# Turning attention probabilities by VectorE and 16 transfers a head in place of TensorE's transposes

## The reference

```python
s = einsum('nbqhd,nbkhd->nbhqk', qb, kk) * HEAD_DIM**-0.5 + bias   # masked to the window
p = exp(s - max(s)); den = sum(p)
o = einsum('nbhqk,nbkhd->nbqhd', p, vv) / den
# groups merged by their denominators, then
y = o * silu(z);  x = x + y @ w_out;  out = rmsnorm(x, final_norm)
```

## Time and profile before

| | us |
|---|---|
| median of 3 runs (1427.52 to 1428.34) | 1427.92 |
| the profiled execution, its time | 1427.84 |
| its span in the trace | 1426.0 |
| TensorE busy in the span | 1414.5 (99%) |
| VectorE / ScalarE / GpSimd busy | 866.0 / 705.3 / 387.2 |

### The profile page before, as it was taken

How to read it: one execution, slowest core, us unless ns; L and a number is a source line. 1 busy time by engine, 2 the same in 40 slices (tenths; PEclk the granted TensorE clock), 3 DMA queues, 4 the chain that set the end, 5 groups by cost and what they waited for, 6 DMA issues and landing times.

```text
span 1426.0 us, 22807 instructions
## 1 busy us (share of the span) xinstructions
PE 1414.5 (99%) x8515; PEld 1256.6 (88%) x8515; DVE 866.0 (61%) x1417; ACT 705.3 (49%) x999; POOL 387.2 (27%) x171
## 2 busy tenths in 40 slices
PE   8999999999999999999999999999999999999997
PEld 8999999988888888888888888888888888888886
DVE  3999999632544444446666666666656666666523
ACT  6444444675644444445454545444444544545543
POOL 6888888888300000000000000000000000001595
PEclk9999999999999999999999999999999999999999
DMA  9766766655757557569676676666577666574662
GB/s 283 195 183 187 195 180 192 193 177 180 242 202 254 201 198 253 196 201 265 191 196 183 172 194 197 184 184 185 164 207 194 177 185 185 161 220 151 229 207 88
DMA packets 401023, 279.06 MB, mean 196 GB/s; under 512 B 6731, under 2 KB 355483, under 8 KB 400588
## 3 DMA queue, kind: packets, MB, share of 16 engines
q1 hardware_dynamic: 400492, 277.47, 65.9%
q10 hardware_dynamic: 480, 0.90, 0.2%
HBM read 267.79 MB, written 10.55 MB: 195 GB/s over the span
## 4 chain that ended last, share of the span: by engine, by line
PE 98%; ACT 1%; DMA 0%; DVE 0%; issue 0%; POOL 0%; POOLq 0%; ACTq 0%
PE bank L423 14%; PE bank L419 14%; PE bank L447 10%; PE bank L449 10%; PE bank L448 10%; PE bank L422 7%; PE bank L420 7%; PE bank L427 6%; PE bank L428 6%; PE bank L429 6%; PE bank L1521 1%; PE bank L1559 1%; PE bank L1413 1%; PE bank L1539 0%; PE bank L1544 0%; ACT mem_a L699 0%
## 5 line engine op out<-in xcount | busy, mean ns | idle before, releaser
L365 POOL TENSOR_TENSOR w_lo<-raw,w_hi 128x1024 fp32r<-128x1024 f32 x159 | 382.7, 2423 | 1013.1 <-ACT w_hi L356 1013.0
L356 ACT ACTIVATE w_hi<-raw 128x1024 fp32r<-128x1024 f32 x254 | 268.4, 1061 | 326.4 <-PE bank L449 192.5
L394 DVE TENSOR_TENSOR w_lo<-raw,w_hi 128x1024 fp32r<-128x1024 f32 x224 | 272.2, 1223 | 111.6 <-ACT w_hi L388 109.1
L388 ACT ACTIVATE w_hi<-raw 128x1024 fp32r<-128x1024 f32 x224 | 236.5, 1058 | 155.1 <-PE bank L423 147.1
L427 PE MATMUL bank<-mem_a,w_hi 128*128 128x256 f32 x768 | 216.1, 281 | 1.8 <-DVE mem_a L1012 1.6
L428 PE MATMUL bank<-mem_a,w_hi 128*128 128x256 f32 x768 | 214.4, 279 | 0.0
L429 PE MATMUL bank<-mem_a,w_lo 128*128 128x256 f32 x768 | 213.4, 278 | 0.0
L423 PE MATMUL bank<-mem_b,w_hi 128*128 128x512 f32 x512 | 202.5, 396 | 0.0
L419 PE MATMUL bank<-mem_b,w_hi 128*128 128x512 f32 x512 | 202.3, 395 | 0.0
L365 DVE TENSOR_TENSOR w_lo<-raw,w_hi 128x1024 fp32r<-128x1024 f32 x96 | 117.6, 1226 | 135.0 <-ACT w_hi L356 134.9
L447 PE MATMUL bank<-w_hi,mem_a 128*128 128x512 f32 x504 | 196.5, 390 | 0.0
(11 more groups left out here) (195 smaller groups left out, 2106.6 us busy)
## 6 DMA issues: line engine op xcount, KB each, us to landing
raw<-b_w_in_dram SPq DMA_DIRECT2D x128, 512.0 KB, 4.3
raw<-w_kv_dram SPq DMA_DIRECT2D x48, 1024.0 KB, 7.0
raw<-w_kv_dram SPq DMA_DIRECT2D x96, 512.0 KB, 5.5
raw<-a_w_in_dram SPq DMA_DIRECT2D x47, 1024.0 KB, 5.8
raw<-a_w_out_dram SPq DMA_DIRECT2D x16, 1024.0 KB, 5.0
raw<-b_w_out_dram SPq DMA_DIRECT2D x16, 1024.0 KB, 5.0
v_dram<-v_stage SPq DMA_DIRECT2D x12, 512.0 KB, 3.4
v_rows<-v_dram SPq DMA_DIRECT2D x15, 384.0 KB, 5.8
```

The lines of the kernel that those rows point to most:

```text
L356: nc.scalar.activation(w_hi[:, stream.half_slot(half), :], raw[:, slot, part:part + HALF], ACT.Copy).then_inc(hi_done, 1)
L365: eng.tensor_tensor(w_lo[:, stream.half_slot(half), :], raw[:, slot, part:part + HALF], w_hi[:, stream.half_slot(half), :].bitcast(F32), A ...
L394: nc.vector.tensor_tensor(w_lo[:, QKV.half_slot(half), :], raw_half(half), w_hi[:, QKV.half_slot(half), :].bitcast(F32), ALU.subtract).the ...
```

## The change

Each 128 x 512 row half of `prob` is transposed by VectorE in squares of 32 by 32 into a new tile `prob_sq`. Squares that lie off the diagonal of a block are then on the wrong partitions; 16 transfers a head (`MOVES`), one for each pair of a source and a destination group of 32 partitions, write them back into `prob` at their place. Each is 32 partitions x 2 halves x 512 bytes, 32 KB. ACT and DVE then make `prob_hi` and `prob_lo` in four pieces of 128 columns from `prob` in SBUF, and TensorE reads the other groups' probabilities from `prob` itself in four runs of 32 columns. `prob_t`, the PSUM copies and the separate `v_last` go. The attention trails by one head less: `attend(h-1)` stands at the end of head h, and two heads are peeled.

```diff
+PEELED = 2
+SQUARE = 32
+SQUARES = P // SQUARE
+MOVES = SQUARES * SQUARES
...
+        def turned_probs(t, block):
+            return prob[:, t, :].rearrange("p (i b s) -> p b i s", i=SQUARES, b=BLOCKS)[:, block, :, :]
...
@@ SP
+            def move_squares(h):
+                sp.wait_ge(squares_turned, TT * (h + 1))
+                for i in range(SQUARES):
+                    for j in range(SQUARES):
+                        row = BLOCKS * SQUARE
+                        sp.dma_start(prob[j * SQUARE:(j + 1) * SQUARE, :, i * row:(i + 1) * row],
+                                     prob_sq[i * SQUARE:(i + 1) * SQUARE, :, j * row:(j + 1) * row]
+                                     ).then_inc(prob_turned, 16)
...
                     load_half(sp, h, half, w[:, tiles, bass.ds(cols[half // 2], P)])
+                    if half == NG:
+                        move_squares(h - 2)
...
                     load_slab(sp, B_OUT, c, q, out_slab(b_w_out[0], c, q))
+                    if (c, q) == (0, 0):
+                        move_squares(HEADS - 2)
                     if (c, q) == (0, B_OUT.per_turn - 1):
-                        sp.wait_ge(attended, HEADS - 2)
-                        load_v(HEADS - 2, (HEADS - 2) * P)
-                        sp.wait_ge(scores_done, HEADS)
-                        sp.dma_start(v_last, v_dram.ap()[:, :, :, (HEADS - 1) * P:]).then_inc(v_last_in, 16)
+                        sp.wait_ge(attended, HEADS - 1)
+                        load_v(HEADS - 1, (HEADS - 1) * P)
+                        move_squares(HEADS - 1)
                         sp.wait_ge(resid_stored, 16)
                         sp.dma_start(resid[:, :, :], resid_dram.ap()).then_inc(resid_in, 16)
@@ ACT: slab step 6 of head h, after copy_lower(h, 3) and before head_hi(h)
+            def probs_hi(h):
+                act.wait_ge(prob_turned, 16 * MOVES * (h + 1))
+                for u in range(TT):
+                    for t in range(TT):
+                        nc.scalar.activation(of_squares(prob_hi[:, u, t * P:(t + 1) * P]),
+                                             turned_probs(t, SAME if t == u else CROSS), ACT.Copy).then_inc(prob_his, 1)
@@ ACT: after head 15
-            y2_his(range(6, last - 2))
+            y2_his(range(6, last - 1))
             copy_lower(last, Z_SLAB)
             tanh_gate(last)
-            copy_probs(last - 1)
-            values_hi(last - 1, v_rows, v_loaded, 16 * last)
             exps(last)
+            y2_his([last - 1])
+            values_hi(last)
             split_hi(act, B_OUT, 0, 2)
-            (y2 and probabilities of heads 13 to 15 between the halves of slab 3)
+            probs_hi(last)
+            split_hi(act, B_OUT, 0, 3)
             y2_his([last])
@@ DVE: slab step 4, after normalise(h-1)
+            def turn_squares(h):
+                positive(dve, prob_turned, 16 * MOVES * h)
+                for t in range(TT):
+                    dve.wait_ge(prob_ready, 2 * h + t + 1)
+                    nc.vector.transpose(prob_sq[:, t, :].rearrange("p (j b s) -> p b j s", j=SQUARES, b=BLOCKS),
+                                        prob[:, t, :].rearrange("p (b j s) -> p b j s", b=BLOCKS, j=SQUARES)
+                                        ).then_inc(squares_turned, 1)
@@ DVE: slab step 6 (Z_SLAB)
                     add_q(h, NG)
+                        values_lo(h - 1)
+                        probs_lo(h - 1)
@@ PE
-            def turn_probs(h): 8 transposes
+            def attend(h):
+                pe.wait_ge(prob_turned, 16 * MOVES * (h + 1))
...
-                        mm = nc.tensor.matmul(bank[7][:, t * P:(t + 1) * P], values[:, g, t, :],
-                                              prob_t[:, g - 1, t, :], start=False, stop=(g, t) == (NG - 1, TT - 1))
+                        mm = nc.tensor.matmul(of_squares(bank[7][:, t * P:(t + 1) * P]), v_rows[:, g, t, :],
+                                              turned_probs(t, g + 1), start=False, stop=(g, t) == (NG - 1, TT - 1))
...
                     out_project(pe, B_OUT, c, q, bank[2 * (c % 2):2 * (c % 2) + 2], y2_in, y2_lo if c == 0 else None)
-                    if c == 0 and q == 1:
-                        attend(last - 1, v_rows)
-                        turn_probs(last)
                     if c == 0 and q == 2:
-                        attend(last, v_last)
+                        attend(last)
```

More of the change, by code:

```diff
@@ L119 @@
 Z_BANK = 6
-PEELED = 3
+PEELED = 2
+SQUARE = 32
+SQUARES = P // SQUARE
+MOVES = SQUARES * SQUARES
 PART = KT * S
@@ L201, in build @@
         prob_hi, prob_lo = sb("prob_hi", [P, TT, S], F32R), sb("prob_lo", [P, TT, S], F32R)
-        prob_t = sb("prob_t", [P, NG - 1, TT, P])
+        prob_sq = sb("prob_sq", [P, TT, BLOCKS * P])
         bias = sb("bias", [P, BLOCKS, P + 1])
@@ L205, in build @@
         z_tanh = sb("z_tanh", [P, S])
-        v_last = k_t[:, :, :].rearrange("p g (t k) -> p g t k", t=TT)
         diag = prob[:, 0, 0:TT * P].rearrange("p (t k) -> p t k", t=TT)
@@ L227, in both_parts, with of_squares @@
             return mem[:, 2 * kt * S:2 * (kt + 1) * S]
+        def turned_probs(t, block):
+            return prob[:, t, :].rearrange("p (i b s) -> p b i s", i=SQUARES, b=BLOCKS)[:, block, :, :]
+        def of_squares(queries):
+            return queries.rearrange("p (i s) -> p i s", i=SQUARES)
         def halves(tokens):
@@ L264, in build @@
         half_in = [sem(f"half_in{i}") for i in range(HEAD_RING)]
-        v_evicted, v_stored, v_loaded, v_last_in = sem("v_evicted"), sem("v_stored"), sem("v_loaded"), sem("v_last_in")
+        v_evicted, v_stored, v_loaded = sem("v_evicted"), sem("v_stored"), sem("v_loaded")
         hi_done, lo_pool, lo_dve, mm_done = sem("hi_done"), sem("lo_pool"), sem("lo_dve"), sem("mm_done")
@@ L302, in build @@
         z_tanh_ready, z_gate_ready = sem("z_tanh_ready"), sem("z_gate_ready")
-        row_maxed, rden_ready, prob_ready, prob_turned, prob_copied = (
-            sem("row_maxed"), sem("rden_ready"), sem("prob_ready"), sem("prob_turned"), sem("prob_copied"))
+        row_maxed, rden_ready, prob_ready, squares_turned, prob_turned = (
+            sem("row_maxed"), sem("rden_ready"), sem("prob_ready"), sem("squares_turned"), sem("prob_turned"))
         attended, y2_ready, y2_hi, y2_lo = sem("attended"), sem("y2_ready"), sem("y2_hi"), sem("y2_lo")
@@ L591, in head_extras @@
                     load_bias(sp.snap(h * (BLOCKS * S)) if stage == PEELED else h * (BLOCKS * S))
-                if stage >= 2:
+                if stage >= 1:
                     if stage == PEELED:
-                        sp.wait_ge(attended, h - 2)
-                    load_v(h - 2, sp.snap((h - 2) * P) if stage == PEELED else (h - 2) * P)
+                        sp.wait_ge(attended, h - 1)
+                    load_v(h - 1, sp.snap((h - 1) * P) if stage == PEELED else (h - 1) * P)
+            def move_squares(h):
[6 more added lines that the diff above has]
+                                     ).then_inc(prob_turned, 16)
             for h in range(PEELED):
@@ L870, in tanh_gate, with values_hi @@
                 nc.scalar.activation(z_tanh[:, :], z_t[:, :], ACT.Tanh, scale=0.5).then_inc(z_tanh_ready, 1)
[L872 to L876, removed]
+            def values_hi(h):
+                act.wait_ge(v_loaded, 16 * (h + 1))
+                nc.scalar.activation(v_hi[:, :, :], v_rows[:, 0, :, :], ACT.Copy).then_inc(v_his, 1)
             def exps(h):
@@ L896, in head_step @@
                     tanh_gate(h - 1)
-                if j == NG and stage >= 2:
-                    copy_probs(h - 2)
                 split_head_hi(act, h, j)
@@ L905, in head_step @@
                     copy_lower(h - 1, j + NG + 1)
-                if j == 5 and stage >= 2:
-                    values_hi(h - 2, v_rows, v_loaded, 16 * (h - 1))
+                if j == 5 and stage >= 1:
+                    values_hi(h - 1)
+                if j == 6 and stage >= 1:
+                    probs_hi(h - 1)
                 if j == 6:
@@ L1220, in head_lo, with values_lo @@
                                         ALU.subtract).then_inc(q_split, 1)
-            def values_lo(h, values):
+            def values_lo(h):
                 dve.wait_ge(v_his, h + 1)
-                nc.vector.tensor_tensor(v_lo[:, :, :], values[:, 0, :, :], v_hi[:, :, :].bitcast(F32),
+                nc.vector.tensor_tensor(v_lo[:, :, :], v_rows[:, 0, :, :], v_hi[:, :, :].bitcast(F32),
                                         ALU.subtract).then_inc(v_split, 1)
             def probs_lo(h):
-                dve.wait_ge(prob_his, h + 1)
-                nc.vector.tensor_tensor(prob_lo[:, :, :], bank[4][:, :].rearrange("p (u s) -> p u s", u=TT),
-                                        prob_hi[:, :, :].bitcast(F32), ALU.subtract).then_inc(prob_split, 1)
+                dve.wait_ge(prob_his, TT * TT * (h + 1))
+                for u in range(TT):
+                    for t in range(TT):
```

(43 more changed lines are left out.)

## The result

The changed kernel takes 1430.85 us (median of 15 runs, 1430.30 to 1431.32) against 1427.74 of before (15 runs): ratio 1.0021, 95% interval 1.0014 to 1.0028. It is 3.1 us slower, where 5.0 us less were forecast.

What follows compares the result with a forecast made beforehand. TensorE, busy 99% of the span, was taken as the bound. Loop gain -13.05, attend(14) moved ahead of T +1.55 and the tail +6.5 gave -5.0 us: 1427.84 to 1422.8 us, forecast's own range 1419.5 to 1425.5, overall 1417 to 1431.

Steps and rivals of the forecast that it cites:

- TensorE's gain in the loop: Head loop: removing TensorE's eight transposes saves 0.87 us a head, 13.05 us over 15 heads.
- T: Start of the output projection's first matmul, 1327.27 before; forecast to come 11.5 us earlier.
- Runs of 32 columns at no cost: TensorE's eight matmuls reading four runs of 32 columns: 0 added to their 0.89 us a head.
- Transposes of 0.65 us: DVE's two 128x512 transposes after normalise: 0.65 us each, 1.3 us a head, hidden in the loop.
- The loop holds, up to 0.86 us a move: Head loop: the new chain stays hidden with 6 us to spare, cost 0; it breaks at 0.86 us a move.
- A move costs 0.46 us: SP's queue: each of 16 moves takes 0.46 us to issue, 7.4 us together, with 0.37 and 0.83 as ends.
- DVE starts the last scores at T + 1.0: After head 15: DVE's bias on the last scores starts at T + 1.0 in place of T + 0.2.
- Chunk 1 at T + 32.5: Output projection: chunk 1 starts at T + 32.5 in place of T + 26.0, 6.5 us later, behind a late slab.
- The page's fixed cost of a transfer: Skill page weighed for the moves: about 2.0 us fixed per transfer, 32 us a head if paid one after another.
- rival 3: After head 15: granted clock falls to 1.2 GHz for one slab of chunk 1, doubling 5.6 us: 1428.4; chance 0.08.
- The mechanism named for the tail: After head 15: chunk 1's first slab, issued behind the moves, lands late, so chunk 1 starts 6.5 us later from T.

Runs made afterwards that it cites:

- x8: e1 plus 8 additional 32 KB transfers a head to HBM, issued ahead of the 16 moves: 1427.15 us, ratio 0.9994 to the kernel before.
- x16: e1 plus 16 additional 32 KB transfers a head to HBM, issued ahead of the 16 moves: 1503.51 us, ratio 1.053 to the kernel before.
- e2: Changed kernel, but SP issues chunk 1's first slab and the residual before head 15's 16 moves: 1422.55 us, ratio 0.9963 to the kernel before.
- e1: Changed kernel, but head 15 alone is transposed by TensorE as before, without its 16 moves: 1414.88 us, ratio 0.9909 to the kernel before.
- e3: Changed kernel, but ACT issues 8 of head 15's 16 moves and SP the other 8: 1425.49 us, ratio 0.9982 to the kernel before.
- g1: e1 plus four additional transfers a head, of different kinds (within SBUF, from HBM, to HBM): 1416.80 us in one run.
- x4: e1 plus 4 additional 32 KB transfers a head to HBM, issued ahead of the 16 moves: 1416.05 us, ratio 0.9915 to the kernel before.

## Why the prediction was wrong

- **TensorE's gain in the loop**: right. It is 13.05 us, and T comes 11.48 us earlier where 11.5 were forecast. (The period before is 43.11 us and not 43.16, which changes nothing.)
- **Runs of 32 columns at no cost**: right, 0.89 us as before.
- **Transposes of 0.65 us**: right, 1.30 for two. The estimate of 1.24 each, from the figure of the Trainium skill in "VectorE: DVE Perf Modes" (The three transpose paths), is too long for this case: 512 columns in float32 took 0.69.
- **The loop holds, up to 0.86 us a move**: right in mechanism. At 0.64 it has 3.7 us to spare, which gives (0.64 + 3.7/16 =) 0.87, and x8 and x16 put the edge at 3.4 to 3.5 us. That the size fits so well is in part luck. The squares landed 1.9 us after the start of the last issue, about 1.1 us sooner than the sum had it, and from there to `q_t` it took 8.5 us (1090.88 to 1099.36) and not 7.5.
- **A move costs 0.46 us**: wrong, and this is the mis-sized term. It measured 0.60 and a gap, 0.64 in the loop; after head 15 the sixteen took 11.0 us, as one of them took 1.43. I took 0.46 from six issues on another queue. I passed over SP's own rows, of the residual (0.64) and of the value rows:

```profile
1324.98 0.57 SPq L585 DMA_DIRECT2D v_rows<-v_dram  x1
```

With 11.0 us in place of 7.4, all that stands behind the moves comes 3.6 us later.
- **DVE starts the last scores at T + 1.0**: wrong, it is T + 2.3. About 0.4 us of this is a slip in the sum: in the earlier trace rows DVE is ready at T - 0.3, and one more remainder (0.8) and TensorE's 0.87 give T + 1.4. For the other 0.9 the traces suggest a cause that no run tests. The moves of head 14 keep ACT waiting, so POOL starts on the first slab at T - 12.3 and not at T - 17.7, and beside it DVE's `q_lo` takes 2.62 us where it took 0.41.
- **Chunk 1 at T + 32.5**: T + 38.1. The two terms before this one put the issue of its slab at T + 21.3 and not at T + 16.5. With 0.3 us of longer landing and 0.4 at the start of the chunk they make the 5.6 us.
- **The page's fixed cost of a transfer**: the Trainium skill gives its 2.0 us in "DMA: Bandwidth & Descriptors" (Anatomy of one DMA) for transfers that GpSimd issues. The moves come from SP, and they landed a median 1.9 us after their issue and overlapped.
- **The clock, given as rival 3 at 0.08**: put at nothing in the sum, wrongly. It fell in both waits and cost 1.9 us after the second. It doubled nine matmuls and not a slab. The sum should have carried it, for the forecast itself had TensorE standing twice. The Trainium skill warns against idle gaps between matmuls in "TensorE: Matmul & The Clock Gate" (Why this matters for your kernels), and these waits agree with it.

Together these are 5.6 + 1.9 = 7.5 of the 7.8 us between forecast and profiled execution. The late chunk alone would have turned the forecast of -5.0 us into +0.6, no change; the clock makes it slower. The mechanism named for the tail, a slab issued behind the moves, is confirmed by e2, and e1 confirms that the whole loss lies there.

## What to carry to other kernels

A change inside a loop is paid at the loop's end, where the next iteration no longer covers its latency: here 13 us were won in 15 heads and 16 lost in the last, and treating the last head the old way keeps them. e2 is the smaller repair: it issues the loads that are free to go while SP stands waiting for the squares. Price an issue by a row of the same kind of transfer on the same queue, because sixteen of them multiply the mistake, and ask what else stands in that queue behind them. Where the sum lets the busiest engine stand for some us, add the lower clock after the wait, and count short waits that stand close together as well.

## What the runs showed of the hardware

- Issues of transfers on SP differ by kind: 0.37 us (a weight half of 512 KB), 0.42 (16 or 32 KB to HBM), 0.57 to 0.60 (16 to 64 KB into `prob` and `probe`, 32 or 128 partitions).
- Sixteen transfers of 32 KB within the SBUF, issued in 10.2 us, each landed a median 1.9 us after their issue, so they overlapped. One that ACT issued 0.3 us after SP's 2 MB residual landed after 8.7 us.
- The granted clock fell to half in waits of TensorE of 9.5 (e3), 6.7, 5.0 and 4.0 us, and in x8 after waits of 0.6 and 1.8 us with eight matmuls between them. It did not fall after single waits of 2.0 us (x8, head 1), 1.3 (g1), 1.0 (x16) and 0.7 (x4).
